# Block inverse of a two-block transformer kernel: where the filling units stand among the levels

## The reference

```
decay = exp(where(causal, gc[..., :, None] - gc[..., None, :], -inf))
a_low = where(strict, einsum("bhnid,bhnjd->bhnij", k_beta, k) * decay, 0.0)
t_mat = a_low + eye(L)
rhs = concatenate([v * beta[..., None], k_beta * exp(gc)[..., None]], axis=-1)
sol = lax.linalg.triangular_solve(t_mat, rhs, left_side=True, lower=True, unit_diagonal=True)
u, w = sol[..., :dv], sol[..., dv:]
# then a scan over the chunks with u, w, q, k
```

## Time and profile before

| | |
|---|---|
| time, median of 3 runs | 969.88 us (969.68 to 971.83) |
| time of the profiled execution | 969.85 us |
| span of the profiled execution | 968.0 us |
| mean granted TensorE clock | 0.998 of full speed |
| TensorE busy | 958.0 us, 99% of the span |
| POOL busy | 742.8 us, 77% |
| ScalarE busy | 511.5 us, 53% |
| VectorE busy | 365.8 us, 38% |
| levels 1 to 5 of the inverse, group 0 and group 1 | from 118.94 to 142.62 us, and from 259.79 to 283.47 us |

### The profile page before, as it was taken

One profiled execution on the slowest core, in us unless ns is written; L12 is line 12 of the kernel. 1 busy time (PEld: TensorE's weight loads), 2 busy tenths in 40 slices (PEclk: granted clock), 3 DMA queues, 4 the chain that ended last, 5 costly groups with the idle time before them and its releaser, 6 DMA issues.

```text
span 968.0 us, 14697 instructions
## 1 busy us (share of the span) xinstructions
PE 958.0 (99%) x5708; PEld 815.1 (84%) x5708; DVE 365.8 (38%) x844; ACT 511.5 (53%) x753; POOL 742.8 (77%) x593
## 2 busy tenths in 40 slices
PE   9999999999999999999999999999999999999997
PEld 8988879988878888888888887899888888888885
DVE  5687625785624245031122245052343241111103
ACT  6576635464644347455354556584566564444431
POOL 5967654876654988899877987778876889888890
PEclk9999999999999999999999999999999999999999
DMA  7746242654434766767644665656565557666541
GB/s 261 216 132 196 89 137 77 181 154 149 132 110 137 255 213 179 237 193 211 202 153 139 211 219 168 233 155 187 182 196 152 152 163 228 182 189 192 179 130 44
DMA packets 76750, 167.33 MB, mean 173 GB/s; under 512 B 8348, under 2 KB 13704, under 8 KB 76552
## 3 DMA queue, kind: packets, MB, share of 16 engines
q1 hardware_dynamic: 71296, 156.40, 53.3%
q10 hardware_dynamic: 5384, 9.99, 3.2%
HBM read 165.32 MB, written 1.05 MB: 172 GB/s over the span
## 4 chain that ended last, share of the span: by engine, by line
PE 97%; DVE 1%; ACT 1%; DMA 0%; issue 0%; DVEq 0%; ACTq 0%
PE L L517 23%; PE L L519 22%; PE L L518 22%; PE Q L519 2%; PE Q L517 2%; PE Q L518 2%; PE L L889 2%; PE L L891 2%; PE L L890 2%; PE Q L734 1%; PE Q L1185 1%; PE L L788 1%; PE L L790 1%; PE L L789 1%; PE Q L852 1%; PE L L827 1%
## 5 line engine op out<-in xcount | busy, mean ns | idle before, releaser
L504 POOL TENSOR_TENSOR w_lo<-raw,w_hi 128x512 fp32r<-128x512 f32 x588 | 741.3, 1299 | 201.7 <-ACT w_hi L1333 201.1
L1333 ACT CAST w_hi<-raw 128x1024 fp32r<-128x1024 f32 x294 | 305.2, 1055 | 244.1 <-PE L L519 106.2
L517 PE MATMUL L<-w_hi,uH 128*128 128x512 f32 (+1 forms) x768 | 305.4, 398 | 0.3
L519 PE MATMUL L<-w_hi,uL 128*128 128x512 f32 (+1 forms) x768 | 296.6, 386 | 0.0
L518 PE MATMUL L<-w_lo,uH 128*128 128x512 f32 (+1 forms) x768 | 296.1, 386 | 0.0
L519 PEld LDWEIGHTS L<-w_hi,uL 128*128 128x128 f32 x768 | 144.3, 188 | 29.8
L517 PEld LDWEIGHTS L<-w_hi,uH 128*128 128x128 f32 x768 | 144.5, 188 | 29.3 <-DVE uL L1949 1.5
L518 PEld LDWEIGHTS L<-w_lo,uH 128*128 128x128 f32 x768 | 144.7, 188 | 26.5 <-issue 0.5
L517 PE MATMUL L<-w_hi,hH 128*128 128x512 f32 x176 | 69.0, 392 | 0.0
L519 PE MATMUL L<-w_hi,hL 128*128 128x512 f32 x176 | 68.6, 390 | 0.0
L518 PE MATMUL L<-w_lo,hH 128*128 128x512 f32 x176 | 68.5, 389 | 0.0
(11 more groups left out here) (367 smaller groups left out, 1288.3 us busy)
## 6 DMA issues: line engine op xcount, KB each, us to landing
raw<-in_w_in SPq DMA_DIRECT2D x88, 512.0 KB, 3.7
raw<-in_w_ffn_gate SPq DMA_DIRECT2D x22, 512.0 KB, 3.7
raw<-in_w_ffn_up SPq DMA_DIRECT2D x22, 512.0 KB, 3.6
raw<-in_w_ffn_down SPq DMA_DIRECT2D x22, 512.0 KB, 3.6
raw<-in_w_gate SPq DMA_DIRECT2D x22, 512.0 KB, 3.7
raw<-in_w_up SPq DMA_DIRECT2D x22, 512.0 KB, 3.7
raw<-in_w_down SPq DMA_DIRECT2D x22, 512.0 KB, 3.5
raw<-in_w_out SPq DMA_DIRECT2D x16, 512.0 KB, 3.6
```

Source lines behind the costliest of these rows:

```text
L504: last = nc.gpsimd.tensor_tensor(lo[:, cc], raw[:, n % RAW, cc], hi[:, cc].bitcast(F32), ALU.subtract)
L517: mm(dst, sH, wH, start=start, stop=False)
L519: return mm(dst, sL, wH, start=False, stop=stop)
L1333: copy(halves[SLOT[u]][0], raw[:, u % RAW, :]).then_inc(w_hi_there, 1)
```

## The change

In levels 1 to 5 the whole unit is issued between X and Y, and nothing between Y and the next level's X. The top level is as before: the half with k = 0 between X and Y, the other in the scan. No instruction is added or left out, and no other engine's list is touched.

```diff
@@ kind == "inv", in the loop over the levels l = 1 to 6, top = (l == 6) @@
                             last.then_inc(*PE.mark(step, "turned", l))
-                        fill(step, l + 1, (0,))
+                        fill(step, l + 1, (0,) if top else None)
                         pe.wait_ge(*VE(step, "X", l))
                         if l > 1:
                             pe.wait_ge(*AC(step, "Td", l))
...
                         last.then_inc(*PE.mark(step, "Y", l))
-                        if not top:
-                            fill(step, l + 1, (1,))
```

## The result

The changed kernel takes 978.18 us (median of 4 runs, 977.65 to 978.46) against 970.82 us for the kernel before (median of 4, 969.68 to 971.83): ratio 1.0076, 95% interval 1.0058 to 1.0093, so slower by 0.8%. The forecast was 978.0. The profiled executions are 977.65 and 969.85 us, 7.8 us apart; the sum of the prediction said 8.1.

The account below looks back on a forecast made before the run. TensorE, busy 99% of the span, was taken to bound the kernel. Per place 1.38 - 0.57 = 0.81 us, ten places 8.1 us, added to 969.85 gave 977.95, forecast 978.0 us, range 976.0 to 981.0.

Parts of the forecast that it names:

- The bound: Whole kernel: TensorE, busy 99% of the span, leads the weight stream, so time added inside the inverse reaches the end.
- The growth between X and Y: Levels 1 to 5, X to Y: six more wide matmuls at 0.23 us add 1.38 us per place.
- changes of kind: Around the half behind Y: slower first matmul and later next X fall away, saving 0.11 + 0.09 = 0.20 us.
- The shrinking behind Y: Start of Y to next X: VectorE's chain leaves 1.64 us instead of 2.21, 0.57 less per place.
- hand-over: VectorE's T update to TensorE's next X: 0.05 us, from hg's transpose; bounds nothing to 0.14 us.
- The sum: Both inverses: 1.38 - 0.57 = 0.81 us more per place, ten places 8.1 us, 977.95 us.
- Edits at nothing: Top level, casts and slots, SyncE's loads, first scan's wait: no cost and nothing given back.
- The wait of the first scan: TensorE's 0.9 us wait for ScalarE's copy, behind the top level's last transposes: claimed to stay 0.9 us.
- The casts' lead of five units: ScalarE's weight casts: five units of lead, so they cannot become late; without that cover, 0.2 us at a time.
- The clock: Both inverses: granted clock stays 1.00; rival of a fall to 1.2 GHz, about 1,006 us, chance 0.03.
- Faster: Behind Y: T is not what X waits for, so 2.0 us are saved, 967.9 us; chance 0.02.
- no change: Behind the inverse: the 8.1 us idle time is made up at later waits; chance 0.02.

Follow-up runs that it names:

- one group: The change made in the inverse of group 1 alone, against the kernel before: 973.84 us against 970.09, ratio 1.0034.
- the mirror: Kernel before with the whole unit of levels 1 to 5 behind Y, nothing between X and Y: 978.01 us against 970.09, ratio 1.0074.
- the third instruction: One extra VectorE instruction ahead of the updates of T: kernel before 969.98 us against 970.09; changed kernel 981.46 against 969.96.
- the first four experiments: Not listed under this name; four runs share the 970.09 us comparison: the mirror, one group, nine and three, and the third instruction in the kernel before.
- four-to-top: Kernel before, group 0's level 5 unit split 4, 4, 4, the last four matmuls in the top level: 968.98 us against 969.96, then 968.88 against 969.91.
- nine and three: Kernel before with nine wide matmuls between X and Y and three behind Y, instead of six and six: 971.05 us against 970.09, ratio 1.0007.
- six instructions: Changed kernel with four extra VectorE instructions ahead of the two updates of T in levels 1 to 5: 1000.59 us, one execution.

## Why the prediction was right

- **The bound.** That TensorE leads the weight stream and that nothing later gives the time back held: one group costs half, and POOL's own wait grew by what TensorE lost (7.7 us).
- **The growth between X and Y.** 12 wide matmuls take 133.61 - 130.69 = 2.92 us with both changes of kind; the sum had 1.56 + 1.38 = 2.94.
- **The shrinking behind Y.** 1.64 us predicted, 1.64 measured, with 0.84 or 0.83 to VectorE's start, 0.75 for the pair and 0.05 to 0.06 for the hand-over. The hand-over was taken from a far row and held; that it can be longer is shown by the mirror (0.14 us ahead of Y), so the bound for it was not idle. Waits of 0.95 us, not 1.0, since a wait on PE is counted from the modelled end of the last matmul.
- **The sum.** 0.79 us a place instead of 0.81: twice 3.95 us from X(1) to X(6), 7.9 against 8.1. That the median, 978.18 us, lies 0.2 us from the forecast is partly luck: the two medians differ by 7.4 us, because two of the four executions of the kernel before lie 2 us above the others. The 7.8 us of the profiled pair are what bears out the sum.
- **Edits at nothing.** The wait of the first scan stayed at 0.9 us, and the wait for low halves stayed at one of 0.2 us. The casts' lead of five units has no row of its own; what the runs show is that no wait for weights came. That this wait hangs on the top level's transposes was shown by the last version, which moved them and lost it.
- **The clock.** 1.00, as forecast. The low chance that I gave to a fall rested on a single stop of 0.86 us, and the clock did fall with stops 2.4 times as long as those of the change: the forecast was right for this size only. (The Trainium skill, "TensorE: Matmul & The Clock Gate", section on psum-queue depth-cycling, has idle times between groups of matmuls swing the clock: not so here at 0.95 us in 5.6, seen at 2.27 us in 6.9 in one of the two inverses.)
- **Faster and no change** fell with the time itself, and the mirror and the third instruction show why: the chain behind Y is there in every kernel, and what hid it was the half unit.

## What to carry to other kernels

Work that fills gaps is worth only what it covers: measure each chain from the instruction that starts it to the one that waits (here 1.64 us behind Y, 2.0 behind X), give each gap that much and no more, and the excess can go where there is still a wait. Merging two fillings into one saves the two changes of kind, 0.20 us here, and costs a chain, 1.0 us. The slack is read from the timeline, end of the chain against start of the waiter; shares of busy time (99% and 98%) tell nothing of it.

## What the runs showed of the hardware

**The clock fell at stops of 2.27 us, but not each time.** Stops of 2.27 us in every 6.9 us left it at its upper level through five levels in group 0 and brought it to the 1.2 GHz level four times in group 1, twice 1.4 to 1.5 us behind the end of a stop and twice within the last 0.4 us of one. Stops of 0.95 and 1.28 us left it up in both groups.

**The times scatter in steps, which the traces place in the first ten microseconds.** The 27 runs of the kernel before that stood beside the first four experiments lie at 969.7 to 970.2, 970.6 to 970.9, and 971.8 to 972.1, with one at 973.2. A profiled execution of the four-to-top kernel in the upper steps (970.86 us) has TensorE waiting 2.2 us at the start where that of the kernel before (969.85 us) has 0.4. First the former's wait and timeline, then the latter's timeline:

```profile
PE Q L967 <- DVE xn L2084: 2.2, 2, 1.4
...
9.87 1.27 POOL L504 TENSOR_TENSOR w_lo<-raw,w_hi 128x512 fp32r<-128x512 f32 x1 [9.43 <-ACT w_hi L1358]
...
10.09 1.19 DVE L2084 TENSOR_SCALAR xn<-x,small 128x256 f32<-128x256 f32 x1
```

```profile
9.70 0.61 DVE L2059 TENSOR_SCALAR xn<-x,small 128x256 f32<-128x256 f32 x2
...
10.00 1.44 POOL L504 TENSOR_TENSOR w_lo<-raw,w_hi 128x512 fp32r<-128x512 f32 x1 [9.56 <-ACT w_hi L1333]
```

Where VectorE gets its two instructions in before POOL starts, they take 0.61 us together; where it comes 0.2 us after, the first alone takes 1.19 and ends 0.14 us behind POOL's. All eleven traces agree: an instruction of this pair that starts ahead of POOL's first takes 0.35 us, one that starts behind it 1.19 to 1.35. In eight traces both start ahead. In that of nine and three one comes late, and X(1) starts at 119.8 us instead of 118.7 to 119.1; in those of the first four-to-top run and of the six instructions both come late, and X(1) starts at 120.9 and 121.0. One late instruction or two are thus the likely origin of the two upper steps, and the 2.2 us ahead of the inverse in the kernel with six instructions. That the two engines get into each other's way on these SBUF operands was not tried by itself. (The Trainium skill, "Advanced Engine Details and Errata", section Mode Summary, says that VectorE's second SBUF port is shared with GpSimd, and that GpSimd's instructions and those of VectorE that use two ports block each other; these rows agree.) The updates of T take 0.75 us with POOL busy throughout or at rest for a part, so they show nothing of it.
